# Dense attention on one core: VectorE takes both heads' maxima of a unit, then its two copies

## What is computed

```python
def dense_attn(q, k, v):
    qg = q.reshape(Bq, Lq, Hk, Hq // Hk, dh)
    s = jnp.einsum('bqkgd,bskd->bkgqs', qg, k).astype(jnp.float32) * (dh ** -0.5)
    p = jax.nn.softmax(s, axis=-1).astype(v.dtype)
    o = jnp.einsum('bkgqs,bskd->bqkgd', p, v)
```

## Time and profile before

| | us |
|---|---|
| runs | 4711.34, 4712.8, 4694.65 |
| median | 4711.34 |
| profiled execution | 4706.8 |
| its span | 4704.9 |
| mean granted clock over the span | 0.937 |

### The profile page before, as it was taken

How to read it: one execution, slowest core, us unless ns; L and a number is a source line. 1 busy time by engine, 2 the same in 40 slices (tenths; PEclk the granted TensorE clock), 3 DMA queues, 4 the chain that set the end, 5 groups by cost and what they waited for, 6 DMA issues and landing times. The chain is left out here.

```text
span 4704.9 us, 49822 instructions
## 1 busy us (share of the span) xinstructions
PE 4047.0 (86%) x19322; PEld 1995.5 (42%) x19323; DVE 1384.7 (29%) x2592; ACT 910.1 (19%) x1940; POOL 121.6 (3%) x199
## 2 busy tenths in 40 slices
PE   5997887998998889889778698998589996888985
PEld 2564664554445554344554333332234443323332
DVE  1576665112205651220562311110321113100114
ACT  2013554002003330210350211111020002111112
POOL 0000000000000000000000000000100000000001
PEclk8998999999999999999898799998799997999997
DMA  6201222000100000001320297789700003998794
GB/s 256 99 36 54 91 108 99 18 36 21 53 36 19 1 10 36 27 27 54 111 112 2 98 393 287 305 331 408 315 18 36 36 18 160 381 413 332 285 397 161
DMA packets 78509, 668.28 MB, mean 142 GB/s; under 512 B 9488, under 2 KB 11352, under 8 KB 44176
## 3 DMA queue, kind: packets, MB, share of 16 engines
q1 hardware_dynamic: 41568, 563.81, 29.7%
q0 software_dynamic: 18128, 67.77, 4.2%
q10 hardware_dynamic: 18656, 34.49, 2.1%
HBM read 610.98 MB, written 55.05 MB: 142 GB/s over the span
## 5 line engine op out<-in xcount | busy, mean ns | idle before, releaser
L235 PE MATMUL banks<-arena 128*128 128x512 f32 (+2 forms) x4544 | 1754.5, 549 | 95.2 <-ACTq L136 74.1
L235 PEld LDWEIGHTS banks<-arena 128*128 128x128 f32 x4544 | 844.6, 192 | 1002.5 <-issue 888.0
L1914 PE MATMUL banks<-arena 128*64 128x512 f32 x3136 | 737.2, 627 | 141.8 <-DMA arena<-in_w_gu 139.4
L1914 PEld LDWEIGHTS banks<-arena 128*64 128x64 f32 x3136 | 232.1, 145 | 637.9 <-issue 460.0
L1931 PE MATMUL banks<-arena 128*64 128x512 f32 x1568 | 347.3, 595 | 0.0
L1155 PE MATMUL banks<-arena 128*64 128x128 f32 x1952 | 158.2, 285 | 82.8 <-DVE arena L1168 43.5
L581 DVE SCALAR_TENSOR_TENSOR arena<-arena 128x1024 f32<-128x1024 f32 x240 | 195.9, 878 | 0.2 <-DVEq L136 0.2
L1931 PEld LDWEIGHTS banks<-arena 128*64 128x64 f32 x1568 | 108.1, 137 | 204.2 <-issue 204.2
L513 ACT ACTIVATE arena<-arena 128x512 f32<-128x512 f32 (+1 forms) x152 | 74.7, 580 | 609.0 <-DVEq L136 608.9
L1984 DVE COPY arena<-banks 128x256 f32<-128x256 f32 x98 | 41.1, 420 | 501.2 <-PE banks L1921 501.2
L277 DVE SCALAR_TENSOR_TENSOR arena<-banks,arena 128x512 f32<-128x512 f32 (+1 forms) x72 | 51.9, 721 | 424.4 <-PE banks L235 424.4
(11 more groups left out here) (292 smaller groups left out, 3030.6 us busy)
## 6 DMA issues: line engine op xcount, KB each, us to landing
arena<-in_w_gu SPq DMA_DIRECT2D x132, 2048.0 KB, 15.0
arena<-in_w_dn SPq DMA_DIRECT2D x66, 2048.0 KB, 11.9
arena<-in_w_ada SPq DMA_DIRECT2D x24, 2048.0 KB, 7.3
y_tok<-arena ACTq DMA_DIRECT2D x196, 128.0 KB, 9.0
y_tok<-arena POOLq DMA_DIRECT2D x1, 16384.0 KB, 45.1
arena<-in_ab_w_ada SPq DMA_DIRECT2D x6, 2048.0 KB, 9.3
arena<-in_cd_w_ada SPq DMA_DIRECT2D x6, 2048.0 KB, 7.3
arena<-in_cd_w_in SPq DMA_DIRECT2D x6, 2048.0 KB, 7.4
```

Source lines behind the costliest of these rows:

```text
L235: last = pe.matmul(bank(g % 8)[:, 0:n], lhsT, rhs, start=k == 0, stop=k == KT - 1)
L1914: last = pe.matmul(bank(2 + s_)[64 * h:64 * h + 64, :], xbT[:, k, 64 * s_:64 * s_ + 64], w_gu[s_][:, k, h], start=k == 0, stop=k == KT - 1 ...
```

## The change

In `dve`, the copies of unit i - 1 leave the loop over the two heads and stand behind it.

```diff
@@ -1177,8 +1177,8 @@
                     for s_ in range(2):
                         if i < n:
                             self.maximum(d, link, i, s_)
-                        for g in copies[s_:s_ + 1] if len(copies) > 1 else copies[:s_]:
-                            self.copy(d, g, "D")
+                    for g in copies:
+                        self.copy(d, g, "D")
                     spare = self.dve_fill
```

## The result

The changed kernel takes 4744.51 us (median of five runs, 4740.16 to 4755.47), the kernel before 4704.94 (five runs, 4694.65 to 4712.8). The ratio is 1.0088, with a 95% interval of 1.0066 to 1.011: **39.6 us slower**. The two runs of before that were added since the prediction moved its median down by 6.4 us. The forecast was 42 us over the median shown then.

A forecast was written before the change was run, and what follows sets the result against it. It took a chain of waits through DVE's first maximum and unbroken ACT work as the bound. Chain 17 plus clock falls 26 made 43 us, 4750, placed at 4753 us as the median lies higher; own range 4738 to 4765.

The forecast's parts named there:

- What bounds the stage: Latent units of A_AB: scores, first maximum on DVE, 4.6 us unbroken ACT work, last value matmuls, next scores; 9.98 us an iteration.
- Copy 1: DVE's copy of group 1 in a latent iteration; predicted to start at 514.91 in place of 513.47, 1.44 us later.
- values 1: PE's value matmuls of group 1, waiting for that group's DVE copy; predicted to start at 515.64 in place of 514.20.
- turn 0: PE's transposes of group 0, starting an iteration at 511.15 in the timeline read.
- Slack of 0.89 us: Part of the 1.44 us delay absorbed by PE's waits for ACT, leaving 0.55 us an iteration, 17 us over 31.
- The gap of 1.90 us: PE's predicted idle time in each iteration between the transposes of group 2 and the value matmuls of group 1.
- The fill's cover: Two convolution steps on DVE would end at 519.2, before the division, possible only after 519.3; nothing charged.
- The clock falls in 6 of 10 iterations: PE's clock drops from 2.4 to 1.2 GHz at the idle gap in 19 of 31 iterations, costing 26 us.
- Price: Cost of one clock fall on PE: 3.41 us at half clock, 1.35 us lost.
- Rival 1: Clock holds in the latent stage and only the chain shifts: +17 us, 4728 us; chance 0.23.
- Rival 2: Clock falls in every latent iteration: 17 + 42 = 59 us, 4770 us; chance 0.12.
- Rival 3: No slower, or faster, as ACT's chain stays the bound in the latent stage: 4690 to 4711 us; chance 0.10.

The follow-up runs named there:

- e4: Kernel before, with DVE copying groups 1 to 4 in units of five groups, ACT only group 0; 4686.98 us beside 4704.12, ratio 0.9956.
- e3: Kernel before, second head's maximum split into two 512-column reductions with the copy of group 1 between, then merged; 4712.35 us beside 4704.12, ratio 1.0012.
- e1: Changed kernel plus 8 extra identity transposes on TensorE before the value matmuls of group 1, which altered the attention output; ratio 0.9989 to before.
- e5: Changed kernel with the transposes of group 2 done three times into the same place; 4722.86 us beside 4701.01 of before, ratio 1.0044.
- e6: Changed kernel with the transposes of group 2 done twice into the same place; 4725.01 us, ratio 1.0050 to before.

## Why the prediction was right, point by point

- **What bounds the stage.** Right. The chain through ACT was the pace: taking copies off it gained 0.66 us an iteration (e4), and the second maximum's earlier factor was worth nothing in the changed kernel.
- **Copy 1 later by 1.44 us, values 1 with it.** Right: 417.19 - 412.70 = 4.49 us behind turn 0, where it was 3.05 (514.20 - 511.15).
- **Slack of 0.89 us, 0.55 us an iteration, 17 us in all.** Right: 10.54 for 9.98 is 0.56, in 30 iterations for the 31 counted, so 16.8 us in the latent part. The prediction gives the slack once as 0.89 us and once, as the bound of a gain, as the 0.69 us of idle time that PE's rows show. The larger one is the slack: values 1 to values 2 took 1.77 us before where 1.17 do without a wait, and values 3 to values 4 took 1.05 for 0.76, together 0.89. e3 shows it from the other side.
- **The gap of 1.90 us.** 1.91 measured. The fill's cover held too: the convolution steps end at 420.75, and the division comes at 421.00.
- **The clock falls in 6 of 10 iterations, 19.** The mechanism was right, the number over by four: 15 falls, two of which lasted twice as long. Price: 24.8 us for 17 times 3.41 us at half clock is 1.46 us each, where 1.35 was worked out. The misses nearly cancel: 26 us forecast, 24.8 measured. That it came so near is in part luck: the share of 6 in 10 was put between none and all from three single waits, and none of the rows gives it.
- **Sum.** 43 us forecast; the latent part of the profiled execution is 41.6 longer, the median 39.6. (4706.8 + 43 + 4.5 would be 4754; the text has 4753. It calls the range +30 to +50 and gives 4738 to 4765, which is +27 to +54. Neither changes the argument.) The span is only 33.4 longer. From the second context unit to the end the changed kernel took 3948.4 us and the kernel before 3956.4; in all ten profiles but that of e1 this rest, whose instructions are the same, lies between 3948.4 and 3960.5. So the 8 us are of the size by which single executions differ, and no effect of the edit is shown there.
- **Rival 1** (the clock holds) needed e5 or e6 to come about. **Rival 2** (every iteration) didn't: 15 of 30. **Rival 3** failed where the text said it would be decided, at ACT's row without idle time.
- **"The granted clock of 500 to 600 us is about 0.9"** was a little low: it is 0.95 there, and 0.92 from 410 to 700.

## What to carry to other kernels

An operation's place on a helper engine is to be judged by who waits for it and with what slack. Here the maximum moved forward had none to give to, and the copy moved back had 0.89 us for a delay of 1.44. A wait of TensorE in dense work has two prices, its length and what the clock does behind it, and the second was the larger here (24.8 us beside 16.8). Where an engine idles at a known place (ACT ahead of its first exponential), work that another engine does on the path belongs there.

## What the runs showed of the hardware

The same wait, of the same helper, repeated 30 times at each of five lengths, let the clock fall 0 times at 1.04, 1.19 and 1.47 us, 10 times at 1.72 and 15 times at 1.91. A fall lasted 3.41 us in all but two cases and cost 1.4 to 1.5 us where matmuls stood densely. The same length of gap fell in one iteration and held in the next. The length alone doesn't decide: a wait of 1.52 us fell in the windowed attention of before, 30 waits of 1.47 us held in e6, where the turn ahead of the wait is twice as long. A wait for streamed weights in the context units fell at 2.12 us in the kernel before and held at 2.65 us in e6, where the 64 matmuls behind it took 1.93 us, with the clock at 1.00 from 775.71 to 790:

```profile
778.69 1.93 PE L432 MATMUL banks<-arena 128*2 128x128 f32 x64 [2.65 <-DMA arena<-in_w_ada]
```

What else decides was not tried. The number of falls need not be the same in each execution, and only one execution of each kernel was recorded.
